# Moving the split of a finished attention block ahead of the next pair's sigmoids and scans

## What is computed

```python
for blk in range(seq // SB_QBLOCK):                 # 4 blocks of 128 queries
    z = einsum('bhqd,bhkd->bhqk', q[lo:hi], k[:hi]) * scale
    log_1m = where(causal, log_sigmoid(-z), 0.0)
    tail = cumsum(log_1m, axis=3, reverse=True) - log_1m
    a = where(causal, exp(log_sigmoid(z) + tail), 0.0)
    outs.append(einsum('bhqk,bhkd->bhqd', a, v[:hi]))
merged = sigmoid(gate_a) * (yA @ w_branch_a) + sigmoid(gate_b) * (yB @ w_branch_b)
```

## Time and profile before

| | us |
|---|---|
| median of 3 runs | 1123.0 |
| the three runs | 1117.66, 1123.0, 1126.99 |
| the profiled execution, its time | 1123.21 |
| the profiled execution, its span | 1121.4 |

### The profile page before, as it was taken

One profiled execution on the slowest core, in us unless ns is written; L12 is line 12 of the kernel. 1 busy time (PEld: TensorE's weight loads), 2 busy tenths in 40 slices (PEclk: granted clock), 3 DMA queues, 4 the chain that ended last, 5 costly groups with the idle time before them and its releaser, 6 DMA issues.

```text
span 1121.4 us, 15663 instructions
## 1 busy us (share of the span) xinstructions
PE 1071.5 (96%) x5374; PEld 871.5 (78%) x5374; DVE 865.8 (77%) x969; ACT 709.8 (63%) x753; POOL 315.1 (28%) x178
## 2 busy tenths in 40 slices
PE   4999999989999989999999999999999999999796
PEld 3878876668888747888888888888888888887475
DVE  6654345552365687999999999999999999996376
ACT  3431235451243426888888888888888888886253
POOL 1000000000005013444444444444444444432421
PEclk9999999999999998999999999999999999999899
DMA  9432222114365357999999999999999999997911
GB/s 325 154 111 75 75 76 75 39 38 150 113 227 213 135 185 267 354 388 388 384 377 383 388 376 392 389 388 386 378 380 375 385 385 372 388 374 214 310 46 57
DMA packets 72572, 294.82 MB, mean 263 GB/s; under 512 B 15312, under 2 KB 18384, under 8 KB 47696
## 3 DMA queue, kind: packets, MB, share of 16 engines
q1 hardware_dynamic: 52944, 256.43, 58.7%
q0 software_dynamic: 19008, 35.71, 12.5%
q10 hardware_dynamic: 576, 2.10, 0.5%
HBM read 283.67 MB, written 44.04 MB: 292 GB/s over the span
## 4 chain that ended last, share of the span: by engine, by line
PE 88%; DVE 6%; DMA 2%; issue 2%; ACT 1%; SPq 0%; DVEq 0%; POOLq 0%; ACTq 0%
PE ps L414 26%; PE ps L416 25%; PE ps L415 24%; PE ps L1504 5%; DVE w_lo L398 2%; PE ps L1954 1%; PE ps L1528 1%; PE ps L729 1%; PE ps L753 1%; PE ps L740 1%; ACT w_hi L393 1%; DMA xg<-h_rows,get_idx 1%; DMA ln_b<-in_ln_in_b 1%; DMA raw<-in_w_out 1%; DVE stick L995 0%
## 5 line engine op out<-in xcount | busy, mean ns | idle before, releaser
L1709 DVE TENSOR_TENSOR w_lo<-gu_raw,w_hi 128x2048 fp32r<-128x2048 f32 x128 | 292.3, 2283 | 5.9 <-ACT w_hi L1594 5.9
L1594 ACT ACTIVATE w_hi<-gu_raw 128x2048 fp32r<-128x2048 f32 x128 | 244.9, 1914 | 3.4 <-DMA gu_raw<-in_moe_w_up 3.4
L414 PE MATMUL ps<-w_hi,xgT_hi 128*128 128x512 f32 x512 | 206.6, 403 | 4.9 <-issue 4.8
L416 PE MATMUL ps<-w_hi,xgT_lo 128*128 128x512 f32 x512 | 201.6, 394 | 0.0
L415 PE MATMUL ps<-w_lo,xgT_hi 128*128 128x512 f32 x512 | 200.9, 392 | 0.0
L1809 POOL DMA_INDIRECT xg<-h_rows,get_idx x64 | 144.7, 2262 | 74.8 <-DVE get_idx L1703 55.1
L414 PE MATMUL ps<-w_hi,act_hi 128*128 128x512 f32 x384 | 154.2, 402 | 3.0 <-DVE w_lo L398 1.6
L1714 DVE TENSOR_TENSOR dn_lo<-dn_raw,dn_hi 128x2048 fp32r<-128x2048 f32 x64 | 146.6, 2291 | 8.0 <-ACT dn_hi L1600 4.5
L416 PE MATMUL ps<-w_hi,act_lo 128*128 128x512 f32 x384 | 150.6, 392 | 0.0
L415 PE MATMUL ps<-w_lo,act_hi 128*128 128x512 f32 x384 | 150.4, 392 | 0.0
L1600 ACT ACTIVATE dn_hi<-dn_raw 128x2048 fp32r<-128x2048 f32 x64 | 122.1, 1907 | 0.0
(11 more groups left out here) (199 smaller groups left out, 1751.0 us busy)
## 6 DMA issues: line engine op xcount, KB each, us to landing
gu_raw<-in_moe_w_gate SPq DMA_DIRECT2D x64, 1024.0 KB, 11.4
gu_raw<-in_moe_w_up SPq DMA_DIRECT2D x64, 1024.0 KB, 11.0
dn_raw<-in_moe_w_down SPq DMA_DIRECT2D x64, 1024.0 KB, 10.9
raw<-in_w_in SPq DMA_DIRECT2D x18, 1024.0 KB, 5.1
h_rows<-x_rows SPq DMA_DIRECT2D x8, 512.0 KB, 5.0
raw<-in_w_out SPq DMA_DIRECT2D x4, 1024.0 KB, 5.6
ple_raw<-in_ple_w_gate SPq DMA_DIRECT2D x4, 1024.0 KB, 10.3
x_rows<-in_x SPq DMA_DIRECT2D x4, 512.0 KB, 10.3
```

The costliest lines, as they stand in the source:

```text
L414: nc.tensor.matmul(out, x_hi, w_hi, start=first, stop=False)
L416: return nc.tensor.matmul(out, x_lo, w_hi, start=False, stop=last)
L1594: nc.scalar.activation(m.w_hi[:, 2 * x.b + half], m.gu_raw[:, 2 * x.b + half], ACT.Copy).then_inc(gu_hi, 1)
L1709: nc.vector.tensor_tensor(m.w_lo[:, 2 * x.b + half], m.gu_raw[:, 2 * x.b + half], m.w_hi[:, 2 * x.b + half].bitcast(F32), ALU.subtract).th ...
```

## The change

`high_yb` on ScalarE and `low_yb` on VectorE are written at the top of a pair's work in place of behind its sigmoids and scans. Nothing is added or removed, and the fourth block's split is untouched.

```diff
         for p in range(NPAIRS + 1):
+            if block_done(p) is not None:
+                high_yb(block_done(p))
             if p < NPAIRS:
                 for s in (2 * p, 2 * p + 1):
...
                     nc.scalar.activation(m.sig_pos[s % 4][:, 0:n], ps[:, Z[s % 2], 0:n], ACT.Sigmoid,
                                          scale=HD ** -0.5).then_inc(sig_ready, 1)
-            if block_done(p) is not None:
-                high_yb(block_done(p))
...
         for p in range(NPAIRS + 1):
+            if block_done(p) is not None:
+                low_yb(block_done(p))
             if p < NPAIRS:
                 for s in (2 * p, 2 * p + 1):
...
                     nc.vector.tensor_tensor(m.sig_pos[s % 4][:, 0:n], m.sig_pos[s % 4][:, 0:n],
                                             m.stick[:, b, 1:n + 1], ALU.mult).then_inc(a_ready, 1)
-            if block_done(p) is not None:
-                low_yb(block_done(p))
```

## The result

Thirteen runs of the changed kernel have a median of 1115.2 us (1112.21 to 1117.37), thirteen of the kernel before 1121.18 us (1117.12 to 1126.99). The ratio is 0.9932, with a 95% interval of 0.9916 to 0.9947. The medians are 6.0 us apart, a quotient of 0.9947; by the ratio the gain is 7.6 us, between 5.9 and 9.4.

The account below looks back on a forecast made before the run. TensorE, busy 96% of the span, was taken as the bound; only its three waits for `ybT_lo` could return. 2.91, 0.90 and 1.92 us sum to 5.73: 1123.21 to 1117.5, forecast 1117.4 us, range 1111.5 to 1123.5 us.

Parts of the forecast that it names:

- What bounds the kernel, and the wait: TensorE, busy 96%, waits at line 753 for `ybT_lo` at pairs 6, 10 and 14; 5.73 us by the starts.
- ScalarE and VectorE: Early `high_yb` (0.64 us) and `low_yb` (0.68 us) nearly fit into idle time, so all three waits go whole.
- The delays of 0.06, 0.17 and 0.28 us: How much later early `high_yb` makes `sig_neg` start on ScalarE, at pairs 14, 10 and 6.
- The room of 1.65 to 1.85 us: Time to spare between the end of early `low_yb` and its last useful moment for line 753, at the three pairs.
- What is late next: Pair 14's products have over 7 us before their transposes; the tightest new limit, VectorE's `merge`, has 1.1 us to spare.
- What survives to the end: Behind the attention, from 257 us on, nothing holds to an absolute time, so all that is saved stays saved.
- The saving given back: Rival, 0.06: the experts' weight stream is the true limit with a start that doesn't move; 1123 us.
- the half-kept wait: Rival, 0.06: something else holds the bank when `ybT_lo` is early, so half of 5.7 us stays; about 1120 us.
- the slower case: Rival, 0.03: the moved instructions delay the next weights at three places, 4.0 us on TensorE's path; 1127 us.
- More than the wait: Rival, 0.05: the 2.84 us wait also loses TensorE clock in most unprofiled executions; 9.1 us gained, 1114.1 us.
- the price of 3.4 us: Work missing in 6.7 us at 1.2 GHz, from a granted clock of 0.88 over 420 to 448 us.

Follow-up runs that it names:

- VectorE's half alone: Only VectorE's `low_yb` moves up, against the kernel before; `high_yb` stays behind the sigmoids. Ratio 0.9929.
- ScalarE's half alone: Only ScalarE's `high_yb` moves up, against the kernel before; `low_yb` stays behind the scans. Ratio 0.9998.
- kernels with two and five `low_yb`: The changed kernel with `low_yb` done twice or five times in a row for the first three blocks; ratios to the kernel before 0.9928 and 0.9962.
- changed, again: The changed kernel once more, no edit, beside the kernel before on the same chip. Ratio 0.9937.
- the trace with the three long waits: The kernel before with `low_yb` done five times in a row for the first three blocks. 1137.04 us, ratio 1.0135.
- the two single traces: One more traced execution each: ScalarE's half alone (1121.63 us); the kernel before, transposes ahead of weighted values at pairs 6, 10 and 14 (1119.8 us).

## Why the prediction was right, point by point

- **What bounds the kernel, and the wait.** Right. The three waits were VectorE's order first of all: VectorE's half alone takes 4.8 of the 5.7 us from the stretch and ScalarE's half alone nothing; the last 0.9 us needs both. The waits come off one by one. To measure from start to start (5.73 us) rather than to take the view's 5.5 us was the better count: the stretch is 5.7 us shorter. The time of 1117.4 us stood on a median of three runs, 1.8 us above that of all thirteen; the same sum from 1121.18 us gives 1115.5, against 1115.2 measured.
- **ScalarE and VectorE.** Right. `sig_neg` starts right behind `ybT_hi`, and the scan at pair 14 still waits for ScalarE. The delays of 0.06, 0.17 and 0.28 us that the prediction worked out for `sig_neg` are a small term that it had too high: set against the last gate matmul of the same pair, `sig_neg` starts at the same distance in both traces at pairs 14, 10 and 6 (2.45 us ahead of it at pair 14: 233.87 - 231.42 before, 231.26 - 228.81 after). `ybT_hi` starts at 228.12 us, 0.11 us ahead of the end of the copies, and is 0.60 us long in place of 0.64. The room of 1.65 to 1.85 us is 1.8 to 2.0 us in the changed trace, and the kernels with two and five `low_yb` bracket it.
- **What is late next.** Right. TensorE has no new wait. `merge` at pair 14 has 1.16 us of idle time in front of it, for a forecast of 1.1 us.
- **What survives to the end.** Right within what the traces can tell: 864.6 us behind the attention before, 864.1 after, with 860.5 to 865.0 over all traces. The spans say the same: a mean of 1119.8 us for the four traces with all three waits whole and 1114.1 us for the three with none, 5.7 us. The saving given back, the half-kept wait and the slower case are out.
- **More than the wait.** Here a step was sized too low. I wrote that the trace doesn't bear out a loss of clock "for a gap of this size", from one execution in which it didn't happen. Of seven traces with a wait of 2.0 or 2.8 us at pair 14 three have it, with 2.8, 1.6 and 1.5 us; of the six with a shorter wait there or none, none has. That the clock can be lost at this length is shown. Its mean, 3 in 7 by 2.0 us, is an estimate of 0.8 us from few traces; with it the sum is 6.5 us, inside the measured 5.9 to 9.4. The timed executions give about the same: beside "changed, again" ten of 24 of the kernel before have a mean clock of 0.987 or less, and their mean is 1124.84 us against 1121.75 us of the others, 3.1 us more; over all four comparisons it is 18 of 71, which by 3.1 us is again 0.8 us. So the price of 3.4 us was near what such an execution shows. What was too high was "in most executions", and with it the time of 1114.1 us; and what one trace couldn't show was that a gap of this size costs nothing.
- **What stays open.** The kernels with short waits gain 1.3 to 3.2 us beyond their stretch by the ratio, 2.2 us in the mean, and 0.8 us explains less than half of that. Each of these figures has an interval of some 2 to 3 us to either side, by the medians the excess is much smaller for three of them, and the low mean clocks of the kernel before vary from comparison to comparison (10 of 24, 2 of 23, 1 of 7, 5 of 17). The traces don't show where the rest would be: behind the attention they are on average 1.7 us longer without a wait of 2 us than with one (864.0 us over six, 862.3 over eight), which points the other way. Nor do the runs separate the length of the wait from its place: the 1.86 us wait at pair 10 lost no clock in any of five traces, but it stands at another pair than the waits that did.

## What to carry to other kernels

When TensorE waits for a bank, look at what stands ahead of the last release in the list of the engine that gives it, not at how fast that engine is: an instruction whose data are complete belongs at the first hole, and its room can be read from the timeline beforehand. Measure a wait on TensorE from start to start against an unheld case. And price a wait of 2 to 3 us on a TensorE that is otherwise busy as its length plus a chance of lost clock (here 3 traces in 7, 1.5 to 2.8 us each), which one trace with a clock of 1.00 doesn't rule out.

## What the runs showed of the hardware that was not expected

- At pair 14 TensorE was at its 1.2 GHz level at or right behind a wait of 2.0 us in one of two traces, and of 2.8 us in two of five; other traces with the same waits kept 2.4 GHz. Waits of 3.73, 4.76 and 5.75 us were followed by it in the one trace that has them, and all four executions of that kernel had mean clocks of 0.982 or 0.983. The Trainium skill's page "TensorE: Matmul & The Clock Gate", section "HAM oscillation — how this bites in real kernels", describes such losses behind idle gaps that are longer than these; by that rule the trace with the three long waits agrees, and the three losses behind 1.96 and 2.84 us go beyond it. Here the measurement decides: at this length the clock was lost in three traces of seven.
- The mean clock of an execution doesn't tell whether the attention lost clock: it is 0.989 in the two single traces that lost it there and 0.990 in the one that didn't. At the experts' start the clock differs by itself, 0.87 to 1.00 over 410 to 450 us in the fourteen traces.
